# Mixing the two softmax maps of differential attention on two engines instead of one

## The reference, cut to what matters

```python
scores = jnp.einsum('bhmqd,bhmkd->bhmqk', q_blk, kt).astype(jnp.float32)
scores = scores + bias[None, :, None]              # ALiBi, causal
p = jax.nn.softmax(scores, axis=-1)
a = p[:, :, 0] - lam * p[:, :, 1]                  # the mix of the two maps
return jnp.einsum('bhqk,bhkv->bhqv', a.astype(vt.dtype), vt)
```

## Time and profile before

| | us |
|---|---|
| median of three runs | 2438.58 |
| span of the profiled execution, first to last instruction | 2433.5 |
| what lies around the span, by the median | 5.1 |
| attention stage, as read here | 755 to 1165 of the span |
| PE busy in 755 to 1160 | 349.05 of 405 |
| DVE busy there | 305.05 |
| ACT busy there | 291.57 |
| POOL busy there | 0.00 |

### The profile page before, as it was taken

How to read it: one execution, slowest core, us unless ns; L and a number is a source line. 1 busy time by engine, 2 the same in 40 slices (tenths; PEclk the granted TensorE clock), 3 DMA queues, 4 the chain that set the end, 5 groups by cost and what they waited for, 6 DMA issues and landing times. The chain is left out here.

```text
span 2433.5 us, 31134 instructions
## 1 busy us (share of the span) xinstructions
PE 2156.2 (89%) x9806; PEld 1632.9 (67%) x9807; DVE 1340.7 (55%) x2350; ACT 1047.5 (43%) x1556; POOL 561.5 (23%) x639
## 2 busy tenths in 40 slices
PE   4999999959895988989799938999999999999980
PEld 3674444428654877777688827888888888888870
DVE  3840666015345877877444377557557867454543
ACT  6101111002313777777322225456556756454543
POOL 0002332004200000000000012445544654443430
PEclk7999999979997999999899958999999999999995
DMA  7113454146117434120434338779788988766737
GB/s 235 34 44 133 143 194 158 39 167 200 42 52 176 90 88 87 40 61 1 137 130 143 108 135 335 257 262 369 250 277 283 392 324 294 239 191 233 263 83 293
DMA packets 136149, 424.75 MB, mean 175 GB/s; under 512 B 29296, under 2 KB 45696, under 8 KB 109440
## 3 DMA queue, kind: packets, MB, share of 16 engines
q1 hardware_dynamic: 102720, 269.74, 32.3%
q0 software_dynamic: 27584, 128.77, 17.5%
q10 hardware_dynamic: 5760, 25.17, 2.5%
HBM read 325.30 MB, written 98.32 MB: 174 GB/s over the span
## 5 line engine op out<-in xcount | busy, mean ns | idle before, releaser
L490 PE MATMUL a_bank<-w_in_chunk,hT 128*128 128x512 f32 x512 | 222.9, 598 | 0.7 <-ACT hT L267 0.7
L490 PE MATMUL a_bank<-hT,w_in_chunk 128*128 128x512 f32 x512 | 220.6, 593 | 0.0
L1650 DVE TENSOR_TENSOR w_down_lo<-w_down_raw,w_down_hi 128x2048 fp32r<-128x2048 f32 x64 | 144.2, 2289 | 124.2 <-ACT w_down_hi L1587 117.4
L302 ACT ACTIVATE proj_out<-a_bank 128x512 f32<-128x512 f32 x64 | 38.2, 597 | 399.7 <-PE a_bank L490 389.9
L882 DVE CUSTOM_DVE_ANT_0 scores<-c_bank,alibi 128x512 f32<-128x512 f32 (+3 forms) x320 | 176.2, 606 | 38.2 <-PE c_bank L995 38.2
L490 PEld LDWEIGHTS a_bank<-w_in_chunk,hT 128*128 128x128 f32 x512 | 128.8, 252 | 93.7 <-issue 63.8
L1021 PE MATMUL c_bank<-v_head,map_T 128*128 128x128 f32 x1088 | 150.5, 283 | 32.2 <-ACT map_T L937 30.9
L490 PEld LDWEIGHTS a_bank<-hT,w_in_chunk 128*128 128x128 f32 x512 | 97.1, 190 | 120.9 <-issue 120.8
L1734 PE MATMUL m_bank<-w_down_hi,hidden_T_hi 128*128 128x512 f32 x392 | 159.9, 408 | 6.8 <-DVE w_down_lo L1650 6.8
L1021 PEld LDWEIGHTS c_bank<-v_head,map_T 128*128 128x128 f32 x1088 | 133.8, 194 | 44.6 <-ACT map_T L937 44.0
L928 ACT ACTIVATE scores<-scores,neg_max 128x128 f32<-128x128 f32 (+15 forms) x128 | 153.4, 1199 | 17.6 <-DVE neg_max L886 17.6
(11 more groups left out here) (388 smaller groups left out, 4681.3 us busy)
## 6 DMA issues: line engine op xcount, KB each, us to landing
w_gate_raw<-in_w_gate_dram SPq DMA_DIRECT2D x64, 1024.0 KB, 7.0
w_up_raw<-in_w_up_dram SPq DMA_DIRECT2D x64, 1024.0 KB
w_down_raw<-in_w_down_dram POOLq DMA_DIRECT2D x64, 1024.0 KB
x_tile<-in_x_dram SPq DMA_DIRECT2D x16, 512.0 KB, 5.3
w_in_chunk<-in_w_in_dram POOLq DMA_DIRECT2D x4, 2048.0 KB, 15.2
qT_d<-xn_tile SPq DMA_DIRECT2D x32, 256.0 KB
kT_d<-xn_tile SPq DMA_DIRECT2D x32, 256.0 KB
q_parts<-qT_d SPq DMA_DIRECT2D x32, 256.0 KB, 4.7
```

The lines of the kernel that those rows point to most:

```text
L302: act.activation(ev[:, n % 4, :], bank[4 + n % PB][:], ACT.Copy, scale=HD ** -0.5 / SLOPES[k // 4] if c == 0 else 1.0).then_inc(ev_done, 1)
L490: last = pe.matmul(bank[4 + n % PB][:], lhsT, rhs, start=kt == 0, stop=kt == KT - 1)
L1650: dve.tensor_tensor(wlo[w][:, halves[i]], raw[w][:, halves[i]], whi[w][:, halves[i]], ALU.subtract).then_inc(lo_done[w], 1)
```

## The change

The lowest 3/8 of a unit's columns, rounded down to whole blocks of 128, are mixed on POOL in two passes, the others on DVE as before. `lower(u)` is 0 for t = 1 and 2, 128 columns for t = 3 to 5, 256 for 6 and 7, 384 for 8 to 10, 512 for 11 to 13, 640 for 14 and 15, and 768 for 16. POOL waits for the scale, multiplies the lower columns of map 1 by it in place, waits for its own product, and adds it to map 0. PE waits for both parts ahead of its first transpose.

```diff
+    lower = lambda u: width(u) * 3 // 8 // P * P
+    lows_before = [0]
+    for u in range(UN):
+        lows_before.append(lows_before[-1] + (1 if lower(u) else 0))
...
+        low_scaled, low_mixed = sem("low_scaled"), sem("low_mixed")
...
+                for u in range(UN):
+                    s, low = u % SLOTS, lower(u)
+                    if low:
+                        pool.wait_ge(scale_step, u + 1)
+                        pool.tensor_scalar(S[:, s, 1, 0:low], S[:, s, 1, 0:low], c2[:, s, 0:1], None, ALU.mult).then_inc(low_scaled, 1)
+                        pool.wait_ge(low_scaled, lows_before[u + 1])
+                        pool.tensor_tensor(S[:, s, 0, 0:low], S[:, s, 0, 0:low], S[:, s, 1, 0:low], ALU.add).then_inc(low_mixed, 1)
...
-                    dve.scalar_tensor_tensor(S[:, s, 0, 0:L], S[:, s, 1, 0:L], c2[:, s, 0:1], S[:, s, 0, 0:L],
+                    low = lower(u)
+                    dve.scalar_tensor_tensor(S[:, s, 0, low:L], S[:, s, 1, low:L], c2[:, s, 0:1], S[:, s, 0, low:L],
                                              ALU.mult, ALU.add).then_inc(mixed, 1)
...
                     if c == 0:
                         pe.wait_ge(mixed, u + 1)
+                        if lower(u):
+                            pe.wait_ge(low_mixed, lows_before[u + 1])
```

## The result

The changed kernel takes 2515.62 us (median of 4 runs, 2513.86 to 2517.03) against 2437.94 (2436.85 to 2438.6): 1.0321 times as long, 95% interval 1.0308 to 1.0333, or 77.7 us more. Forecast were 2463.6 us and a range that ended at 2490. Slower was right; the loss is three times the size given.

What follows compares the result with a forecast made beforehand. The prediction took the attention loop's length from scale to first transpose and third score chunk as the bound; delays of 6.1 us a head, about 25 us in all, gave 2433.5 + 25 + 5.1 = 2463.6 us, range 2443 to 2490.

Steps and rivals of the forecast that it cites:

- What bounds the kernel: Attention stage: the length from the scale's end to the unit's first transpose and third score chunk counts; lengthening beyond slack adds up.
- S: The end of a unit's scale on DVE, from which the prediction measures the length to the first transpose.
- Part 1: DVE's mix shrinks to 0.22 + 1.04 us per thousand columns, 23.5 us less busy; worth at most 12.8 us.
- Part 2: POOL's two passes: add 0.19 + 2.11 us per thousand columns, multiply taken at 0.83 per thousand.
- Part 3: POOL's first pass waits for DVE's part of the mix to end; both passes then run full speed beside the score pass.
- rival 2: POOL's multiply runs at the add's rate, exclusion as forecast: 27.6 us more, 2491 us; chance 0.13.
- the list by unit: Forecast delay of each attention unit, 0.1 to 1.8 us; 6.1 us a head, about 25 us in all.
- Part 4: Cost by unit after slack: 0.3 us at t = 15, 1.8 at t = 16, t = 5 hidden under the norm in heads 2 to 4.
- The clock: PE's granted clock in the attention stage, 0.98, could fall with longer pauses at heads' ends: 0 to 3 us, none taken.
- the sum as forecast: Delays of all units over four heads: 24.4 us, with 0.4 for the first head about 25 us.
- the 5.1: Time around the profiled span of 2433.5 us, added to the forecast span of 2458.5 to give 2463.6 us.

Runs made afterwards that it cites:

- probe: Kernel before with POOL passes put ahead of it, DVE idle, then two pairs side by side; at 768 columns the multiply took 2.20 us, a copy 0.82.
- dve_one_col: Changed kernel with DVE mixing a single column beside POOL, the upper columns left unmixed; stage 437.0 us, +25.1 on before (whole 2442.79 us, not comparable).
- copy_for_multiply: Changed kernel with POOL's multiply replaced by a copy of the same columns, their scaling left out; stage 427.0 us, +15.1 on before (whole 2451.08 us).
- warm_half: Changed kernel with 1 to 12 unread matmuls in most units on PE while it waits for the mix; 2504.54 us, 1.0269 of before.
- pool_first: Changed kernel with a 0.15 us DVE write and wait ahead of DVE's mix, so POOL's multiply begins first; 2459.45 us, 1.0091 of before.

## Why the prediction was wrong

**What bounds the kernel: right.** The length from S to the first transpose is what counts, and it adds up over the units: every kernel above moved by it. Counted from the first scale, the last one came 73 us later after the change, 17 to 20 us more with each head.

**Part 1, DVE's share: right** (1552 ns at 1280), and the waits for `max_part` are gone.

**Part 2: the step that failed.** It was "I take 0.83, since the multiply too streams one input", and the real slope is 2.5 us per thousand, beyond the upper end, 2.11, too. The row it was taken from, an affine select, was no multiply. And "the only fp32 multiply", with 16 columns, wasn't the only one: the row of 1264 ns at 510 columns, which the prediction calls an add here and in Part 3, is by the kernel's line 552 a two-input multiply. So a multiply at 2.11 per thousand stood in the rows, and spoke for rival 2. The add proved to have the same rate (1801 ns at 768), the one-input multiply a higher one. With 5.376 thousand lower columns a head the missing 1.67 us are 9.0 a head, 36 in all. With it the list by unit comes out, measured from the unit's scale to the next, against the same distance before: at t = 11 to 13, 0.57 + 0.86 = 1.43, measured 1.43 to 1.44; at t = 14, 0.7 + 1.07 = 1.8, measured 1.8; at t = 8 and 10, 0.3 + 0.64 = 0.94, measured 0.97 to 0.99; at t = 7, 0.1 + 0.43, measured 0.52. At t = 3 and 6 it falls short: 0.5 and 0.7 due, 0.76 and 0.93 measured. Rival 2 named this cause with too small a price: its 27.6 us took the add's rate, and by the measured one its own columns give 36. That the multiply's form is the cause is shown by `probe`, `dve_one_col` and `copy_for_multiply`.

**Part 3: right for this kernel, its reason half wrong.** POOL's first pass stood until DVE's end, and both its passes ran unhindered beside the score pass (1.00 us for 384 columns at 1056.47). But "Who is first matters little ... the lengths add up either way" fell: with POOL first the stage is 55 us shorter, as the multiply holds DVE for 0.84 us per thousand columns and not for its 2.5. For a copy the lengths do add up. The forecast's order held only because DVE's pass began 0.06 to 0.07 us ahead of the multiply.

**Part 4, the units where I had left slack.** At t = 15 I forecast 0.3 of 1.5 us, the rest hidden under ACT's exponential. The cover was for the short length: 1.37 was due with the slower multiply, 2.39 came, of which `warm_half` took 0.8 back. At t = 16, 1.8 + 1.28 = 3.1 was due and 2.9 to 4.0 came; at t = 5 of the heads with a norm 0.9 to 1.9 came, where I had the norm covering it. The granted clock of these three units was 0.77, 0.85 and 0.77, against 0.87, 1.00 and 1.00 before, so part of this is the clock's. What each part comes to is not told apart.

**The clock.** Forecast was "0 to 3 us, of which I take none"; by the estimate above it is 11 to 13. The longer pauses brought it: 3.2 us stood at t = 15 where the slower multiply alone made 1.07 of it. With the copy in its place the granted clock over the stage is 0.95, with the multiply 0.92. It isn't all one cause, since the copy doesn't bring back the 0.97 of before either.

**The account.** 25 (the sum as forecast) + 36 (the multiply) + 11 to 13 (the clock, an estimate) = 72 to 74 of 79. The two units t = 9 (heads 2 and 4) that took 1.1 us more than those of heads 1 and 3 belong to the clock, as their granted clock of 0.80 shows. The remaining 5 to 7 lie at t = 3, 5, 6, 15 and the heads' ends; which mechanism each has stays open, and 2 or 3 us of it may be the difference between two executions. That `pool_first` gives back 55 of the 79 and leaves 24 doesn't contradict this: the same loss is cut another way. The base was off as well, though without effect on the verdict: every later run shows 1.5 to 1.9 us around its span, so the 5.1 was mostly the difference between two executions.

## What to carry to other kernels

Price an operation by a row of the same operation and operands: two one-input passes on one engine, a copy and a multiply, differed threefold. A loop that ends in a fixed order is paid at the first consumer, so ask for each part where it is first needed, not where the whole is; POOL's slow passes cost 79 us ahead of the first chunk, and ahead of the last, on about half the columns, the stage gained 4. And before a second engine is called in, try the first engine's own pass in two parts: that gave the best time here, without the other engine.

## What the runs showed of the hardware

- POOL's multiply by a value per row, fp32: 0.61, 1.24, 2.20 us at 128, 384, 768 columns; by a constant 2.13 at 768; as a two-input multiply with the value spread 1.47; a copy 0.82; a two-input add 1.80. The cheapest form of the product wasn't tried in the kernel.
- DVE's pass with two SBUF inputs, once running, stopped POOL's multiply (2.20 us for 1.24) and add (1.74 for 1.00) to its end. POOL's instruction, once first, made that pass longer by an amount that goes with POOL's columns alone: an add by 2.1 us per thousand (1.74 for 0.89 at 384), a copy by 0.83 (1.48 for 1.15), and the multiply, which lasts 2.5, by only 0.84 (1.77 for 1.42 at 512). A pass begun 0.7 us into a multiply of 768 columns lost nothing (1.55).
- Who is first, when both wait for the same semaphore: POOL's instructions recorded 0.03 to 0.045 us behind DVE's went first (all 56 copies, 55 of 56 adds), those at 0.049 (one add) and 0.06 to 0.07 (all 56 multiplies) were stopped. Whether the form plays a part too wasn't tested.
